# The first block of a two-block transformer kernel reordered: modulation sums on VectorE and GpSimd, the recurrence first, a weight group beside each attention head

## What is computed

```python
mod = (silu(c) @ w_mod + b_mod)                      # 1024 x 6144
shift_m, scale_m, gate_m, shift_f, scale_f, gate_f = split(mod, 6)
h = rms_norm(x, norm_mix) * (1 + scale_m) + shift_m
qa, ka, va, xr, yr, qc, kc, vc, g_logits = split(h @ w_in)
o_a = swa_attention(rms_norm(qa), rms_norm(ka), va, sinks, bias_a)   # 8 heads, window 128
o_b = rg_lru(causal_dwconv(xr, ...), ...) * gelu(yr)                 # gated linear recurrence
o_c = moba_attention(rms_norm(qc), rms_norm(kc), vc, bias_c)         # 8 heads, causal
g = sigmoid(g_logits).reshape(s, 3, 1024)
merged = g[:, 0] * (o_a @ wb_a) + g[:, 1] * (o_b @ wb_b) + g[:, 2] * (o_c @ wb_c)
x = x + gate_m * (merged @ w_out)
h = rms_norm(x, norm_ffn) * (1 + scale_f) + shift_f   # then w_up, conv, w_down
```

## Time and profile before

| quantity | value |
|---|---|
| time, median of 3 runs | 2481.92 us (2480.28 to 2484.15) |
| profiled execution, its span | 2478.1 us |
| share of the median outside that span | 3.8 us |
| PE / DVE / ACT / POOL busy | 94% / 68% / 54% / 1% of the span |
| PE's first dense matmul | 58.86 us |
| first w_out matmul (end of the changed part) | 455.73 us |

### The profile page before, as it was taken

The page is one execution under the profiler, slowest core; times in us unless marked ns, Lnnn a source line. Parts: engine busy times, 40 slices in busy tenths (PEclk is TensorE's granted clock), DMA queues, the critical chain, the costliest instruction groups (busy, mean ns, idle before and its releaser), DMA issues.

```text
span 2478.1 us, 35477 instructions
## 1 busy us (share of the span) xinstructions
PE 2327.6 (94%) x14343; PEld 2038.1 (82%) x14343; DVE 1686.5 (68%) x1755; ACT 1338.1 (54%) x1306; POOL 31.1 (1%) x69
## 2 busy tenths in 40 slices
PE   7999999899988888998988889999999999999997
PEld 3955779899988888998988768888888888888886
DVE  2423555578479655544975378888888888888885
ACT  3323534356353444444544267677767776777674
POOL 1000000000000000000000000000000000000000
PEclk9989999899999999999989889999999999999998
DMA  8524375565654435656434079999999999999993
GB/s 265 162 71 131 128 237 181 143 171 179 179 159 138 136 86 141 182 171 182 149 116 143 32 245 371 333 376 328 367 331 375 320 376 336 368 322 375 333 377 118
DMA packets 413848, 565.79 MB, mean 228 GB/s; under 512 B 15763, under 2 KB 267291, under 8 KB 413691
## 3 DMA queue, kind: packets, MB, share of 16 engines
q1 hardware_dynamic: 411323, 556.67, 66.3%
q0 software_dynamic: 2080, 5.77, 0.9%
q10 hardware_dynamic: 288, 1.05, 0.1%
HBM read 562.37 MB, written 1.08 MB: 227 GB/s over the span
## 4 chain that ended last, share of the span: by engine, by line
PE 84%; DVE 11%; ACT 3%; issue 1%; DMA 1%; SPq 0%; ACTq 0%; DVEq 0%
PE pair L967 58%; PE misc L967 13%; PE pair L1024 3%; DVE arena L1770 3%; DVE wlo L1496 2%; PE misc L1366 1%; PE pair L1377 1%; DVE work L1519 1%; PE misc L1401 1%; PE misc L1126 1%; PE misc L1125 1%; ACT whi L554 1%; PE misc L1033 1%; PE misc L1278 1%; DVE rt L1517 0%
## 5 line engine op out<-in xcount | busy, mean ns | idle before, releaser
L1966 DVE TENSOR_TENSOR wlo<-raw,whi 128x2048 fp32r<-128x2048 f32 x338 | 770.1, 2290 | 124.1 <-ACT whi L898 123.0
L898 ACT CAST whi<-raw 128x2048 fp32r<-128x2048 f32 x338 | 647.2, 1918 | 202.5 <-PE pair L967 101.1
L967 PE MATMUL pair<-hh,whi 128*128 128x256 f32 x1840 | 531.2, 289 | 43.3 <-DVE hl L1510 30.6
L1496 DVE TENSOR_TENSOR wlo<-raw,whi 128x2048 fp32r<-128x2048 f32 (+1 forms) x170 | 384.9, 2265 | 262.4 <-ACT whi L554 261.8
L967 PE MATMUL pair<-hl,whi 128*128 128x256 f32 x1840 | 526.9, 286 | 0.0
L967 PE MATMUL pair<-hh,wlo 128*128 128x256 f32 x1840 | 526.8, 286 | 0.0
L967 PE MATMUL pair<-whi,oph 128*128 128x512 f32 (+1 forms) x1024 | 394.9, 386 | 4.5 <-DVE wlo L1966 2.5
L967 PEld LDWEIGHTS pair<-hh,whi 128*128 128x128 f32 x1840 | 360.2, 196 | 46.8 <-issue 46.4
L967 PE MATMUL pair<-wlo,oph 128*128 128x512 f32 (+1 forms) x1024 | 387.0, 378 | 0.0
L967 PE MATMUL pair<-whi,opl 128*128 128x512 f32 (+1 forms) x1024 | 386.4, 377 | 0.0
L967 PEld LDWEIGHTS pair<-hl,whi 128*128 128x128 f32 x1840 | 360.1, 196 | 0.3
(11 more groups left out here) (372 smaller groups left out, 2534.8 us busy)
## 6 DMA issues: line engine op xcount, KB each, us to landing
raw<-in_moe_w_gate_dram SPq DMA_DIRECT2D x114, 1024.0 KB, 7.3
raw<-in_moe_w_up_dram SPq DMA_DIRECT2D x112, 1024.0 KB, 7.4
raw<-in_moe_w_down_dram SPq DMA_DIRECT2D x112, 1024.0 KB, 6.9
raw<-in_w_in_dram SPq DMA_DIRECT2D x38, 1024.0 KB, 5.4
raw<-in_w_mod_dram SPq DMA_DIRECT2D x24, 1024.0 KB, 5.4
raw<-in_w_up_dram SPq DMA_DIRECT2D x44, 512.0 KB, 4.8
raw<-in_w_xkv_dram SPq DMA_DIRECT2D x16, 1024.0 KB, 5.4
raw<-in_ffn_w_gate_dram SPq DMA_DIRECT2D x22, 512.0 KB, 4.0
```

Of the source, the lines that this page charges most:

```text
L898: act.copy(whi[:, q, :], raw[:, r, :]).then_inc(sem("hi_ready"), 1)
L967: ins = pe.matmul(out_, lhs, rhs, start=start and i == 0, stop=stop and i == 2)
L1496: dve.tensor_tensor(wlo[:, i % SPLIT, 0:size], raw[:, s % RAW, 0:size], whi[:, i % SPLIT, 0:size].bitcast(F32), ALU.subtract).then_inc(sem ...
L1966: dve.tensor_tensor(wlo[:, q, :], raw[:, r, :], whi[:, q, :].bitcast(F32), ALU.subtract).then_inc(sem("lo_ready"), 1)
```

## The change

The w_mod slots leave PE. The first 8 are summed by DVE with a chain of eight instructions of 256 columns per slot, the other 16 by POOL with eight multiplications of 256 columns and three additions of 1024, 512 and 256. PE keeps `mod_columns`, which now also sums over the 128 partitions. The ring for the first block and the dense part of the second has four slots (`RING = 4`); the other two slots of `raw` hold the recurrence's tiles. The order of the groups is now w_mod (8), xr and yr, qa, ka, qc, kc, va, vc, then g, with the 16 w_mod slots strewn among them, then branch_b, branch_ac, w_out. The recurrence's decay and scan run beside the qa to kc groups. Each of the 16 heads has one whole dense group (12 of g, 4 of branch_b) where half a w_mod slot was. Gates are kept as tanh of half the logit, and (tanh + 1) times the branch is halved at the end. The attention's output has one PSUM bank instead of two, and `spread_roots` three banks instead of four.

```diff
 RAW = 6
+RING = 4
...
+    modulator(8)
+    for j in range(4):
+        dense("xr", w_in, [(XR + j * 256, 256)], "act")
+        modulator(j % 2)
...
+    for i in range(12):
+        j, b = divmod(i, 3)
+        dense("g", w_in, [(GL + b * D + j * 256, 256)], "act")
+        modulator(i % 2)
...
@@ gpsimd @@
+            def mod_slot(j):
+                n = mod_slots[j]
+                pool.wait_ge(sem(f"landed{n % RING}"), landed_at[n])
+                if j >= 10:
+                    pool.wait_ge(sem("mod_columns"), j - 1)
+                terms = raw[:, n % RING, :]
+                for c in range(DC):
+                    row = terms[:, c * 256:(c + 1) * 256]
+                    pool.tensor_scalar(row, row, cact[:, c:c + 1], None, ALU.mult).then_inc(sem("pool_terms"), 1)
+                for step, wide in enumerate((1024, 512)):
+                    pool.wait_ge(sem("pool_terms"), 10 * (j - 8) + DC + step)
+                    pool.tensor_tensor(terms[:, 0:wide], terms[:, 0:wide], terms[:, wide:2 * wide], ALU.add)
...
+                pool.tensor_tensor(macc[:, j % 2], terms[:, 0:256], terms[:, 256:512], ALU.add).then_inc(sem("mod_summed"), 1)
+            for j in range(8, 16):
+                mod_slot(j)
+            pool.wait_ge(sem("rnn_ob_lo"), 2)
...
             for h in range(NHEAD):
                 if h >= 2:
                     pool.wait_ge(sem("att_scores"), h - 1)
                 pool.dma_start(bias_buf[h % 2], bass.AP(bias_dram.tensor, h * 512, [[1, P], [P, 2], [1, P]]))\
                     .then_inc(sem(f"bias_landed{h % 2}"), 16)
+                if h % 2:
+                    mod_slot(16 + h // 2)
...
@@ tensor @@
             def mod_columns(j):
-                pe.wait_ge(sem("mod_row"), j + 1)
+                pe.wait_ge(sem("mod_summed"), j + 1)
...
                 if h + 2 < NHEAD:
                     scores(h + 2)
-                mod_half(8 + h // 2, h % 2, 2 if h >= 4 else 0)
+                if h < 12:
+                    dense_group(beside[h], hh, hl)
+                else:
+                    dense_group(beside[h], oph, opl, chunk0=4)
                 pe.wait_ge(sem("att_pt_sb"), h + 1)
+                if h % 2 and h < 15:
+                    mod_columns(15 + h // 2)
...
@@ vector @@
+            def mod_slot(j):
+                n = mod_slots[j]
+                dve.wait_ge(sem(f"landed{n % RING}"), landed_at[n])
...
+                    if c == 0:
+                        ins = dve.tensor_scalar(macc[:, j % 2], row, cact[:, 0:1], None, ALU.mult)
+                    else:
+                        dve.wait_ge(sem("mod_terms"), (DC - 1) * j + c)
+                        ins = dve.scalar_tensor_tensor(macc[:, j % 2], row, cact[:, c:c + 1], macc[:, j % 2], ALU.mult, ALU.add)
```

More of the change, by code:

```diff
@@ L108, in plan, with modulator @@
     w_in = w["w_in"][0]
[L109 to L112, removed]
-    dense("ka", w_in, [(KA, 64), (KA, 64), (KA + 64, 64), (KA + 64, 64)], "act")
[L114 to L117, removed]
+    mods = iter(range(24))
+    def modulator(n=1):
+        for _ in range(n):
+            j = next(mods)
+            dense("mod", w["w_mod"][0], [(j * 256, 256)], None)
@@ L118, in plan @@
+    dense("kc", w_in, [(KC, 256)], "act")
+    modulator()
+    dense("kc", w_in, [(KC + 256, 256)], "act")
     dense("va", w_in, [(VA, 128)], "act")
+    modulator()
     for j in range(2):
         dense("vc", w_in, [(VC + j * 256, 256)], "act")
[L121 to L126, removed]
@@ L224, in build_program @@
         hl = sb("hl", [P, DC, T], F32R)
+        with nc.sbuf_tensor("opf", [P, 2, 24 * T], F32) as opf:
+            pass
         oph = sb("oph", [P, 24, T], F32R)
@@ new lines, in _, with decay @@
+            ahead_of(stage_groups["qa"][0])
+            gates(DC - 2)
+            gates(DC - 1)
+            def decay(half):
+                act.wait_ge(sem("rnn_ix"), 4 * half + 4)
+                for u in range(4 * half, 4 * half + 4):
+                    act.wait_ge(sem("rnn_r"), u + 1)
+                    act.activation(wmul[half][:, u % 4], xrp[:, u, 3:3 + T], ACT.Tanh, scale=coef[:, u:u + 1]).then_inc(sem("rnn_tanh"), 1)
+                for u in range(4 * half, 4 * half + 4):
+                    act.wait_ge(sem("rnn_tanh"), u + 1)
+                    act.activation(xrp[:, u, 3:3 + T], xrp[:, u, 3:3 + T], ACT.Exp, scale=coef[:, u:u + 1])\
+                        .then_inc(sem("rnn_a"), 1)
@@ L619, in _, with inner, hidden_out @@
+            def inner(half):
+                act.wait_ge(sem("rnn_w"), 4 * (half + 1))
+                act.activation(wmul[half], wmul[half], ACT.Sqrt, scale=-1.0, bias=consts[:, 1:2]).then_inc(sem("rnn_mult"), 1)
+            def hidden_out(half):
+                act.wait_ge(sem("rnn_ob"), half + 1)
+                act.copy(oph[:, 4 + 4 * half:8 + 4 * half, :], work[:, 4 * half:4 * half + 4, :]).then_inc(sem("rnn_ob_hi"), 1)
             tiles = [("qa", qa), ("ka", ka), ("qc", qc), ("kc", kc)]
@@ L726, in _ @@
-            for j in range(4):
-                for b in range(3):
-                    ps = group(next(gi))
-                    if j >= 2:
-                        act.wait_ge(sem("merged_f"), j - 1)
-                    act.activation(g_sig[:, j % 2, 2 * b:2 * b + 2, :], ps, ACT.Sigmoid).then_inc(sem("act_read"), 1)
-                gb_ = stage_groups["branch_b"][j]
-                ahead(first_slot[gb_] + 2)
+            for j in range(4):
+                ahead_of(stage_groups["branch_ac"][j])
@@ L1181, in _ @@
-            mod_columns(23)
-            pe.wait_ge(sem("rnn_ob_lo"), 2)
-            gi = iter(stage_groups["g"])
-            for j in range(4):
-                for b in range(3):
-                    dense_group(next(gi), hh, hl)
-                g = stage_groups["branch_ac"][j]
+                o = att_bank(i)
+                pe.matmul(o[half], v[:, 0], pt_buf[h % 2][:, 0:T], start=True, stop=False)
+                pe.matmul(o[half, P:T], v[:, 1], pt_buf[h % 2][:, T:384], start=False, stop=True).then_inc(sem("att_o"), 1)
```

522 lines of the change are left out of this document (273 added, 249 removed).

## The result

The changed kernel takes 2607.88 us (median, 2606.01 to 2610.43), the kernel before 2482.26: a ratio of 1.0507, interval 1.0494 to 1.0519. That is 5.1% slower, 118 us above the forecast of 2490 and far beyond its range. The first w_out matmul comes at 580.08 us, 124.4 later than before and 116 later than I had it. From there to the end of the span (2603.8) it is 2023.7 us, before 2022.4. So all of the loss lies in the part that the change touches.

What follows compares the result with a forecast made beforehand. PE was taken as the engine everything waits for. Its pieces to the first w_out matmul, 62.7 + 58.0 + 1.5 + 72.9 + 241.5 + 23.0 + 4.5 = 464.1 us against 455.73, gave 2490 us, range 2470 to 2512.

Steps and rivals of the forecast that it cites:

- The start: Up to PE's first dense matmul: DVE's sums at 3.9 us per slot, PE starting at 62.7 us, 3.9 later.
- Recurrence and projections: From PE's start to the attention: xr and yr 58.0 us, convolution 1.5, nine groups qa to vc 72.9.
- a rival with 6 to 12 us and a chance of 0.12: In yr to kc, DVE waits for POOL additions and three groups slip: 6 to 12 us, about 2498; chance 0.12.
- The decay and scan lie beside these groups at no cost: Groups qa to vc: the recurrence's DVE work is covered by dense groups; without cover it would cost 40 us.
- My named test: Sign for sharing between DVE and POOL: it counts if the yr groups are more than 9 us apart.
- the ring of four is enough there: Work after the first w_out matmul: four slots leave three groups (17 us) for a transfer of 5.8 us.
- The attention: The 16 heads: 32.7 us, six two-head cycles of 32.1 with PE waiting for a bias, and 16.2; sum 241.5.
- X = 7.0: Length in us of one POOL w_mod slot in the attention; bounds 4.0 and 9.4, each us worth 6 us.
- the bias transfer 3.2: Attention, six times in series behind POOL's slot: a bias load takes 3.2 us from issue to landing.
- the rival's number without a stall: Attention: the bias is there when PE asks; two heads 19.6 us, 75 us less, 2415; chance 0.08.
- Its first instruction waits for the columns that PE makes: Attention: POOL's slot waits for columns from an odd head's end, as the sum has two buffers; six times.
- The end: After the attention: four branch_ac groups 23.0 us, then a 4.5 us wait for the merge before w_out.

Runs made afterwards that it cites:

- e6_late_wait: Changed kernel with POOL's wait for the columns moved from the head of a slot to just ahead of its last addition: 2513.75 us.
- e3_bias_act: Changed kernel with the sixteen bias loads issued from ACT's queue instead of POOL's, all sums kept: 2536.37 us.
- e4_direct: Changed kernel with slots 8 to 23 summed on PE straight into columns, 16 one-column matmuls per slot, and none on POOL: 2529.43 us.
- e10_empty_macc4: Changed kernel with four sum buffers instead of two and all 16 later w_mod slots emptied to the last short addition: 2427.39 us (0.9775 to the kernel before).
- e1_empty_all: Changed kernel with all 16 later w_mod slots kept in place, but POOL doing only the last 256-column addition of each: 2478.05 us.
- e7_macc4: Changed kernel with four sum buffers instead of two, so a slot waits only for the columns of four slots before: 2461.67 us.
- e13_wide_mult: Changed kernel with each slot's eight multiplications done by one POOL operation of 2048 columns, factor broadcast, two sum buffers: 2569.65 us.

## Why the prediction was wrong

**The start** was right: 62.7 forecast, 63.31 measured, from a 3.9 us slot that took 3.9.

**Recurrence and projections** failed by 56 us (132.4 forecast, 188.6 measured). The step that failed is a term put at nothing: the sum 58.0 + 1.5 + 72.9 gives POOL's slots no price at all. Nine of them, 8 to 16, run there in the trace. I saw that about seven would, and priced only what they do to DVE, as a rival with 6 to 12 us and a chance of 0.12. That they hold ring slots appears nowhere. The runs give for slots 8 to 15 29 to 32 us of holding and 16 to 19 of work beside DVE. e6_late_wait gives 15 us back (236.6): POOL waits for columns 28.4 us in all ahead of the first scores, with a raw slot held, and there the multiplications need not wait. The last 8 us are there with empty slots too (203.1 against 195.1), 6.1 of them as a wait of PE for the roots of the normalisation, and were not followed up. "The decay and scan lie beside these groups at no cost" is therefore right to within these 8 us. My named test, yr groups over 9 us apart, came true (107.76 to 125.73), but it doesn't tell sharing from holding: ahead of the late group ACT waits for a weight load, not for DVE.

```profile
122.51 1.90 ACT L610 CAST whi<-raw 128x2048 fp32r<-128x2048 f32 x1 [8.75 <-DMA raw<-in_w_in_dram]
```

The sentence "the ring of four is enough there" was meant for the time after w_out and is right for it; I never asked the same of the time before.

On sharing, the Trainium skill (SBUF — State Buffer, Who interferes with whom) says that a two-input DVE instruction and a GpSimd one that reads SBUF shut each other out for their whole length. The trace agrees: a split takes 2.29 us alone and 4.44 beside POOL, and POOL's two wide additions, 3.68 alone, take 5.70 beside it.

```profile
74.87 5.70 POOL L540 TENSOR_TENSOR raw<-raw 128x1024 f32<-128x1024 f32 x2
...
74.98 4.44 DVE L1546 TENSOR_TENSOR wlo<-raw,whi 128x2048 fp32r<-128x2048 f32 x1
```

**The attention** failed by 51.3 us (241.5 forecast, 292.8 measured, to the first branch_ac matmul at 544.72) in the size of terms; the mechanism was right. "X = 7.0" measured 11.7 and lies above my upper bound of 9.4. Of its pieces the additions took 3.68 + 0.72 = 4.40 us, where I had 3.5. The multiplications are the larger error: 0.90 us for each 256 columns, where I took 0.39 and at most 0.69. My two rows were of operations with a constant; these take a factor for each partition, and whether that makes them dearer no run tells. The term "the bias transfer 3.2" measured 6.0: SP issues 2 MB of weights and then 1 MB of w_mod in the moment in which the slot ends, so that the bias travels beside them. Where the bias is issued apart from such a burst its median over all 16 loads is 3.1 (e3_bias_act), 3.3 (e4_direct) and 3.3 (e10_empty_macc4), against 6.6 here; no run changes this alone, so it is likely, not shown. These two give 4.7 + 2.5 = 7.2 us for two heads (the 2.5 is 6.0 less 3.2 and the 0.3 of hops), 39.2 where I had 32.1, and 43 us for six. The other 8 us are the last copy, 1.3 forecast and 9.50 measured: the w_branch loads stood behind slot 23 in the ring, which ended at 533.10 as SP's row shows, and ACT cast them ahead of the last output. Where that slot is empty (e1_empty_all) or is done early (e7_macc4), the wait is 1.00.

```profile
533.12 3.45 SPq L446 DMA_DIRECT2D raw<-in_w_branch_dram  x6
```

That the slot's length passes through is shown by e13_wide_mult, and the rival's number without a stall (19.6 for two heads, 2415 in all) by e10_empty_macc4 (19.4 and 2427). "Its first instruction waits for the columns that PE makes" is the sentence on which the whole loss in the attention hangs; e7_macc4 shows it by taking the wait away.

By my estimate from the Trainium skill (GPSIMD Engine Reference, section 3.1) the three additions were to take about 4.3 us, and the trace has 4.40. Its one-input rule of about a cycle per column, which made 7.8 in all for X, doesn't hold for these multiplications: 0.90 us per 256 columns.

**The end** failed by 8 us: 35.4 from the first branch_ac matmul to w_out, against 27.5. I took 23.0 for the four groups at PE's pace, but DVE merges one only every 7.5 us: five operations of 0.69, a split of 2.29 and 1.8 of waits for ACT between them, all in series:

```profile
571.84 0.69 DVE L1808 SCALAR_TENSOR_TENSOR opl<-arena,oph 128x512 fp32r<-128x512 f32 x1 [0.70 <-ACT oph L795]
579.33 0.69 DVE L1808 SCALAR_TENSOR_TENSOR opl<-arena,oph 128x512 fp32r<-128x512 f32 x1 [0.69 <-ACT oph L795]
```

No run tried this part by itself. The four errors, 0.6, 56.2, 51.3 and 7.9 us, make the 116.

## What to carry to other kernels

When work moves to an engine that was idle, ask of it not only how long it takes but what it holds meanwhile: the buffer that it reads, its queue, and whoever waits for either. Two more buffers for results of 256 columns were worth 146 us here, and moving one wait past work that didn't need it 94; making the slot shorter by a third was worth 38 with two buffers and nothing with four. And an operation that no row shows should be priced by a row of the same kind, or with a bound wide enough for another kind: the upper bound here was 9.4 us and the slot took 11.7.

## What the hardware showed unexpectedly

- On GpSimd eight multiplications of 128x256 by a factor for each partition take 7.21 us, and one product of 128x2048 with the factor broadcast takes 3.60.
- On PE 16 products of 128 columns and 16 of one column with a 128x128 weight take the same 3.65 and 3.63 us, but the granted clock is 0.95 with the first and 0.78 with the second over the same 160 us.
- A transfer of 128 KB took 3.2 us from issue to landing in the median, and 6.0 in the attention of the changed kernel, where most are issued in the same moment as 3 MB of weights.
